# The heads' output projection in a hybrid decoder layer: input sums made two groups ahead and kept in DRAM

## The reference

```python
x = layer_norm(concatenate([meta, x_prompt]), ln_in_g, ln_in_b)
q, k, v, qi, wi, ki, hq, kf, hi, log_f, hg = project(x, w_in)
attn_o = attention of each query over its top-k keys       # 8 heads of 128
hg_o   = gated linear recurrence, normed and gated         # 8 heads of 128
mix = concatenate([attn_o, hg_o]) @ w_out
x = layer_norm(ALPHA * x + mix, ln1_g, ln1_b)
x = layer_norm(ALPHA * x + swiglu(x, w_gate, w_up, w_down), ln2_g, ln2_b)
```

## Time and profile before

| | |
|---|---|
| median of the runs | 2655.04 us (2654.91 to 2656.0) |
| the profiled execution | 2640.65 us |
| its span from the first to the last instruction | 2639.2 us |
| PE busy | 2543.4 us, 96% |
| DVE busy | 1577.6 us, 60% |
| ACT busy | 973.5 us, 37% |

### The profile page before, as it was taken

The page is one execution under the profiler, slowest core; times in us unless marked ns, Lnnn a source line. Parts: engine busy times, 40 slices in busy tenths (PEclk is TensorE's granted clock), DMA queues, the critical chain, the costliest instruction groups (busy, mean ns, idle before and its releaser), DMA issues.

```text
span 2639.2 us, 47668 instructions
## 1 busy us (share of the span) xinstructions
PE 2543.4 (96%) x20523; PEld 2479.1 (94%) x20523; DVE 1577.6 (60%) x2221; ACT 973.5 (37%) x1550; POOL 173.7 (7%) x198
## 2 busy tenths in 40 slices
PE   5999999999999899989999999999999799999996
PEld 5989999999999888989999999999999799999995
DVE  5157767776656631578777777777777433333345
ACT  5244333343333421345444444444444321212123
POOL 1111111111000112000000000000000000000002
PEclk9899999999999999989999999999999899999997
DMA  4422323333222323243333333343333543433221
GB/s 133 106 56 82 96 80 94 92 88 89 81 73 73 93 87 93 67 142 111 123 106 127 114 119 124 109 129 113 120 116 110 189 157 117 130 101 109 89 67 65
DMA packets 289965, 275.27 MB, mean 104 GB/s; under 512 B 8184, under 2 KB 266536, under 8 KB 289256
## 3 DMA queue, kind: packets, MB, share of 16 engines
q1 hardware_dynamic: 282448, 250.92, 30.7%
q0 software_dynamic: 7344, 21.80, 2.7%
HBM read 245.41 MB, written 27.29 MB: 103 GB/s over the span
## 4 chain that ended last, share of the span: by engine, by line
PE 92%; DVE 4%; ACT 3%; issue 1%; DMA 1%; SPq 0%; DVEq 0%; ACTq 0%
PE acc L1773 47%; PE acc L1373 29%; PE b L1773 5%; PE b L1357 2%; PE acc L1395 1%; PE b L1518 1%; PE b L1636 1%; PE b L1611 1%; PE b L1534 1%; PE b L1715 1%; PE b L1693 1%; PE b L1546 1%; DVE lnd L2360 1%; DMA stg<-hid_dram 1%; PE b L1637 0%
## 5 line engine op out<-in xcount | busy, mean ns | idle before, releaser
L1373 PE MATMUL acc<-xh,wh 128*128 128x260 f32 (+2 forms) x2144 | 456.5, 295 | 10.0 <-DVE xl L2234 4.5
L1373 PE MATMUL acc<-xl,wh 128*128 128x260 f32 (+2 forms) x2144 | 439.8, 287 | 0.0
L1373 PE MATMUL acc<-xh,wl 128*128 128x260 f32 (+2 forms) x2144 | 439.1, 287 | 0.0
L1230 ACT ACTIVATE ph<-pair 128x1024 fp32r<-128x1024 f32 x252 | 267.3, 1061 | 414.1 <-PE acc L1773 405.7
L1773 PE MATMUL acc<-hh,dh 128*128 128x260 f32 x1408 | 399.6, 284 | 14.8 <-DVE dl L2509 11.3
L2371 DVE TENSOR_TENSOR pl<-pair,ph 128x1024 fp32r<-128x1024 f32 x252 | 308.7, 1225 | 159.1 <-ACT ph L1230 159.1
L1773 PE MATMUL acc<-hl,dh 128*128 128x260 f32 x1408 | 399.4, 284 | 0.0
L1773 PE MATMUL acc<-hh,dl 128*128 128x260 f32 x1408 | 399.1, 283 | 0.0
L1373 PEld LDWEIGHTS acc<-xh,wh 128*128 128x128 f32 (+1 forms) x2144 | 335.1, 191 | 17.2 <-DVE xl L2234 5.6
L1373 PEld LDWEIGHTS acc<-xl,wh 128*128 128x128 f32 (+1 forms) x2144 | 336.9, 191 | 0.0
L1373 PEld LDWEIGHTS acc<-xh,wl 128*128 128x128 f32 (+1 forms) x2144 | 336.6, 191 | 0.0
(11 more groups left out here) (442 smaller groups left out, 4495.0 us busy)
## 6 DMA issues: line engine op xcount, KB each, us to landing
raw<-in_w_in_dram SPq DMA_DIRECT2D x52, 1024.0 KB, 5.7
draw<-in_w_down_dram SPq DMA_DIRECT2D x32, 1408.0 KB, 6.5
pair<-in_w_gate_dram SPq DMA_DIRECT2D x42, 1024.0 KB, 5.4
pair<-in_w_up_dram SPq DMA_DIRECT2D x42, 1024.0 KB, 5.1
raw<-in_w_out_dram SPq DMA_DIRECT2D x16, 1024.0 KB, 5.6
hid_dram<-hid SPq DMA_DIRECT2D x22, 520.0 KB, 3.2
stg<-hid_dram SPq DMA_DIRECT2D x44, 260.0 KB, 6.6
x_dram<-sacc SPq DMA_DIRECT2D x4, 1040.0 KB, 4.2
```

The costliest lines, as they stand in the source:

```text
L1230: act.activation(ph[n % 3][:, :, :], block_of(q, i), ACT.Copy).then_inc(sem("h_split"), 1)
L1373: ins = mm(acc[0:rows, t.odd, half, 0:n_], a, b[:, kx0 + k, lo + half * n_:lo + half * n_ + n_], start=(k == 0 and n == 0), stop=(k == kt ...
```

## The change

- The sums move to the end of VectorE's iterations of groups 1 and 2 in stage B, one for each of the eight products. They write two buffers `xs`, which lie where the samples' row work lies later. A sum from the third on waits until the store of the one two before has landed. The waits for the stored states go from group 3 to the first of them, as `xs` lies over those tiles; `sample_rows` waits for all eight stores.
- SP stores each sum to a new DRAM tensor `x_dram`, one after each weight load of groups 2 and 3. After the third weight load of D1 it brings the tensor back to `sacc` in two pieces of four tiles, each when those four are subtracted, the second when the first has landed.
- In D1 a tile then takes two steps: ScalarE rounds all eight, VectorE subtracts all eight. `add_mix` scales by ALPHA as it adds, for the tiles 8 to 15.
- ScalarE rounds ahead of block 11's probabilities, and takes the last product of stage B (`take(3, 3)`) behind both.
- On TensorE `pv(11)` goes behind the first product of D1, and the scores of block 12 behind the first tile of the second. The turns of block 12 stay where they are.

```diff
--- before.py
+++ after.py
@@ -280,8 +280,7 @@
     work = rb.take("work", [NS, 4, KEEP_S])
     vnew = rb.take("vnew", [NS, NG, P])
     assert rb.pos <= R_START + 29248
-    tmp = rb.take("tmp", [P, 2, NT])
-    assert rb.pos <= R_START + 33408
+    xs = at("xs", [P, 2, 2 * LIVE], F32, rb.pos - 8512)
     qpad = at("qpad", [P, NG, NS, NH], F32, R_START + 33408)
     knew = at("knew", [P, NG, NS], F32, R_START + 34432)
     assert R_START + 34432 + 128 <= TOP
@@ -393,6 +392,7 @@
     SUMS, SQ, MU, RSTD, LND = (ssum1, ssum2), (sq1, sq2), (mu1, mu2), (rstd1, rstd2), (lnd1, lnd2)
     x1_dram = nc.dram_tensor("x1_dram", (KD, P, 2 * LIVE), F32, kind="Internal")
     hid_dram = nc.dram_tensor("hid_dram", (FF // P, P, 2 * LIVE), F32, kind="Internal")
+    x_dram = nc.dram_tensor("x_dram", (8, P, 2 * LIVE), F32, kind="Internal")
     ytok = at("ytok", [P, NB + 1, D], F32, 0)
 
     acc = ctx.enter_context(nc.psum_tensor("acc", [P, 2, 2, 512], F32))
@@ -534,15 +534,30 @@
         head_loads(At(0), None)
         with sp.Fori(1, NH, 1) as h:
             head_loads(At(0, 4, h), h)
+        def keep_x(k):
+
+            sp.wait_ge(sem("x_sum"), k + 1)
+            if k:
+                sp.wait_ge(sem("x_kept"), 16 * k)
+            sp.dma_start(x_dram[k], xs[:, k % 2, :]).then_inc(sem("x_kept"), 16)
+
         for g in range(NG):
             for j, c in enumerate((W_COLS["k"] + P * g, W_COLS["v"] + P * g, 2 * P * g, 2 * P * g + P)):
                 s = At(S_B + 4 * g + j)
                 load(s, raw_at(s, KD, P), w_in3[:, :, c:c + P])
+                if g >= 2:
+                    keep_x(4 * (g - 2) + j)
         for n in range(8):
 
             s = At(S_D1 + n)
             c = (n * 256 + 1024) % D
             load(s, raw_at(s, 8, 256), wo3[:, 8:16, c:c + 256])
+            if n == 2:
+                for c4 in range(2):
+                    sp.wait_ge(sem("x_kept"), 128 + 16 * c4)
+                    sp.wait_ge(sem("mix_in"), 4 * c4 + 4)
+                    sp.dma_start(sacc[:, 8 + 4 * c4:12 + 4 * c4, S0:NT], x_dram[4 * c4:4 * c4 + 4].rearrange("k p n -> p k n"))\
+                        .then_inc(sem("x_kept"), 16)
         with sp.Fori(0, 4, 1) as n2:
             for i in range(2):
                 s = At(S_D2 + i, 2, n2)
@@ -1119,16 +1134,12 @@
                         keep_new(g - 1)
                     if j in (1, 2):
                         kv_rows(g, j - 1)
-                    att_probs(n)
+                    if n < 11:
+                        att_probs(n)
 
 
         def mix_round(k):
-            act.wait_ge(sem("x_sum"), k + 1)
             act.activation(xh[:, 8 + k, S0:NT], sacc[:, 8 + k, S0:NT], ACT.Copy).then_inc(sem("mix_h"), 1)
-
-        def mix_resid(k):
-            act.wait_ge(sem("mix_in"), k + 1)
-            act.activation(sacc[:, 8 + k, S0:NT], tmp[:, k % 2, S0:NT], ACT.Copy, scale=ALPHA).then_inc(sem("resid"), 1)
 
         def sample_att(b):
             act.wait_ge(sem("sg_turned"), b + 1)
@@ -1147,13 +1158,10 @@
         for n in range(8):
             if n == 0:
                 act.wait_ge(sem("mm"), T_D1)
-                mix_round(0)
-                for k in range(1, 9):
-                    if k < 8:
-                        mix_round(k)
-                    mix_resid(k - 1)
-                    if k == 3:
-                        take(3, 3)
+                for k in range(8):
+                    mix_round(k)
+                att_probs(11)
+                take(3, 3)
             split(At(S_D1 + n + 1))
             if n <= 4:
                 att_take(11 + n)
@@ -1724,7 +1732,12 @@
                 if n == 0 and i == 0:
                     side = {k: (mix_in(k + 1),) for k in range(7)}
                 if n <= 3:
-                    if i == 0:
+                    if n == 0 and i == 0:
+                        side[7] = (lambda: pv(11),)
+                    elif n == 0:
+                        side[0] = (lambda: att_scores(12),)
+                        side[7] = (lambda: p_turn(12),)
+                    elif i == 0:
                         side[3] = side.get(3, ()) + (lambda n=n: pv(11 + n),)
                         side[5] = side.get(5, ()) + (lambda n=n: att_scores(12 + n),)
                     else:
@@ -2195,6 +2208,11 @@
                 last = V.tensor_scalar(lg[:, hd, 0:w], lg[:, hd, 0:w], nmx[:, 1, hd:hd + 1], None, ALU.mult)
             last.then_inc(sem("att_p"), 1)
 
+        def x_sum(k):
+            if k >= 2:
+                dve.wait_ge(sem("x_kept"), 16 * (k - 1))
+            V.tensor_tensor(xs[:, k % 2, :], fr(xh[:, 8 + k, S0:NT]), fr(xl[:, 8 + k, S0:NT]), ALU.add).then_inc(sem("x_sum"), 1)
+
         q = 3 * (NH - 1)
         for g in range(NG):
             for j in range(4):
@@ -2215,20 +2233,19 @@
                         if q < KEEP_S // 8:
                             take_sample(4 * q, idx[:, 8 * q:8 * q + 8])
                             q += 1
-                    if g == 3 and j == 2:
+                    if g == 1 and j == 0:
                         dve.wait_ge(sem("sstate_out"), 16 * NH)
                         dve.wait_ge(sem("state_out"), 16 * NH)
+                    if g < 3:
+                        x_sum(4 * (g - 1) + j)
+                    if g == 3 and j == 2:
+                        dve.wait_ge(sem("x_kept"), 128)
                         sample_rows()
                     if g == 3 and j == 3:
                         dve.wait_ge(sem("rows_turned"), 1)
                         V.tensor_copy(grow[:].rearrange("p k b -> p (k b)"), b7[:, 0:16]).then_inc(sem("grow_ready"), 1)
 
 
-        def x_sum(k):
-            if k >= 2:
-                dve.wait_ge(sem("resid"), k - 1)
-            V.tensor_tensor(tmp[:, k % 2, S0:NT], fr(xh[:, 8 + k, S0:NT]), fr(xl[:, 8 + k, S0:NT]), ALU.add).then_inc(sem("x_sum"), 1)
-
         def mix_rest(k):
             dve.wait_ge(sem("mix_h"), k + 1)
             V.tensor_tensor(xl[:, 8 + k, S0:NT], sacc[:, 8 + k, S0:NT], fr(xh[:, 8 + k, S0:NT]), ALU.subtract).then_inc(sem("mix_in"), 1)
@@ -2238,7 +2255,13 @@
             t = At(T_D1 + 2 * n + i)
             m = (2 * n + i + 8) % KD
             dve.wait_ge(sem("mm"), (t + 1).v)
-            V.tensor_tensor(cut(sacc[:, m, S0:NT]), cut(sacc[:, m, S0:NT]), alive(t), ALU.add).then_inc(sem(f"acc_read{t.odd}"), 1)
+            dst = cut(sacc[:, m, S0:NT])
+            if n < 4:
+                dve.wait_ge(sem("x_kept"), 128 + 16 * (m // 4 - 1))
+                V.scalar_tensor_tensor(out=dst, in0=dst, scalar=ALPHA, in1=alive(t), op0=ALU.mult, op1=ALU.add)\
+                    .then_inc(sem(f"acc_read{t.odd}"), 1)
+            else:
+                V.tensor_tensor(dst, dst, alive(t), ALU.add).then_inc(sem(f"acc_read{t.odd}"), 1)
 
         def sample_att(b):
             dve.wait_ge(sem("slog"), b + 1)
@@ -2251,10 +2274,7 @@
 
         for n in range(8):
             if n == 0:
-                x_sum(0)
                 for k in range(8):
-                    if k < 7:
-                        x_sum(k + 1)
                     mix_rest(k)
             split(At(S_D1 + n + 1))
             if n >= 1:
```

## The result

The changed kernel takes 2638.24 us (median of 20 runs, 2628.91 to 2653.44). The kernel before, timed beside it on the same chip, takes 2658.37 (20 runs, 2641.76 to 2662.71).

A forecast was written before the change was run, and what follows sets the result against it. TensorE, busy for 96% of the span, bounds the kernel. 2.3 us (earlier start) and 6.0 (inside the ring) make 8.3, other parts nothing; off the median 2655.04 that gives 2646.7, range 2644.4 to 2650.2.

The forecast's parts named there:

- Start: Step to the output projection: rounding may begin at 871.78, first matmul 1.45 us later, 0.34 after the turns end.
- TensorE's line: Output projection: no wait after the first tile; turns of block 12 done at 889.32, before it was 897.59.
- Block 12: Attention block 12: its ScalarE and VectorE line ends by 886.5, TensorE wants it at 888.62; 2.1 us of slack.
- Sums: Eight sums of 0.70 us moved into groups 1 and 2: cost nothing, 0.36 left; uncovered 5.6 in all.
- Restoring: Stored sums' return to `sacc`: landed by 883.9, first needed by `add_mix(0,0)` at 886.5; cost nothing, 2.6 us left.
- Rival B: Start of the output projection: TensorE at the lower clock loses 2.5 us; gain 5.8, time 2649.2; chance 0.07.
- C: Block 12 becomes the bound: split as late as 884, turns wait 3.8 us, gain 4.5, time 2650.5; chance 0.09.
- D: Restored tiles late at `add_mix(0,0)`: free up to 13.5 us landing, at 27.1 slower by 5.3, 2660.3; chance 0.05.
- the sum: Whole kernel: the step's gain of 8.3 us taken off the median of 2655.04, giving 2646.7.
- the ring: Output projection before: eight tiles each sum, round, subtract and scale before `tmp` is free; TensorE waits, clock 0.72 over 873 to 879.
- the 6.0: Output projection: 6.0 us of the 8.3 gained from waiting, refilling and the lower clock inside the ring.
- the 2.3 of the earlier start: Output projection: first matmul at 873.23, not 875.55; 2.3 us of the 8.3.

The follow-up runs named there:

- keeping one wait: Changed kernel with block 11's probabilities ahead of the eight roundings again, so TensorE waits longer at the step's start: 2647.29 us (12 runs).
- the delay: Changed kernel with twelve extra tiles of full matmuls ahead of the output projection's first tile: 2650.17 us (11 runs).
- one tile shorter: Kernel before with one of 16 feature tiles left out of each of the twelve products of groups 1 to 3: 2646.41 us (7 runs).

## Why the prediction was wrong

**The steps held.** *Start*: rounding begins 0.2 us after the turns of block 11; the first output matmul comes 1.42 us later (1.45 forecast), after a wait of 0.37 (0.34). *TensorE's line*: no wait for `xl` after that, clock 1.00; the second weight tile starts at 893.05, 17.5 us after those turns began (17.5 forecast; 25.8 in the first trace of before). *Block 12*: its probabilities are ready at 890.86, 1.84 before TensorE turns them (2.1 forecast). *Sums*: VectorE's idle time before the split that had 1.06 is now 0.26 (0.36 forecast), still ended by ScalarE. *Restoring*: issued at 879.06; the two transfers took 5.1 us (median) to land, where 8.8 was taken, and VectorE goes from block 12's probabilities into `add_mix` at 890.78 without a wait. Rival B (low clock at the start), C (block 12 the bound) and D (restored tiles late) did not come. (C was priced 0.5 us too high: with a split at 884 its line of 7.89 would end at 891.9, 3.3 us behind 888.62 and not 3.8.)

```profile
695.69 2.29 DVE L1884 TENSOR_TENSOR wl<-raw,wh 128x2048 fp32r<-128x2048 f32 x1 [0.26 <-ACT wh L815]
```

**The step that failed is the sum:** "the gain is a length of waiting and of engine work, so I take it off the median". The 8.3 was read from one execution, 2640.65, that stood 0.5% below the median of the three runs beside it. The prediction saw that distance and set it aside. It was the key: the first trace shows the ring at clock 0.72 for 6 us, and the usual execution shows it at 0.50 for 15. The mis-sized term is the 6.0 for "waiting, refilling and the lower clock inside the ring": it measures 10.0 there, which with the 2.3 of the earlier start makes 12.3, not 8.3. With the sample stage steadied, the runs give 10.6 for the change. The range failed with it: its 1 us for the spread of the runs was that of three runs (2654.91 to 2656.0), while the 75 runs of before on record, these three among them, span 2640.75 to 2664.33.

**The second term was missing:** the sample stage, 101.5 us in the first trace and up to 118.4 in others of either kernel, stood in no line of the sum, as it takes no part in the change. Taking its two-column rows apart gains 13.4 us on the kernel before and 7.3 on the kernel after (means of 6 against 75 runs, and 12 against 30). So the kernel after loses some 6 us less in it. That divides the 16.8 us between the means of the two kernels into 10.6 for the step and some 6 for the sample stage; it is a division by these runs and no separate proof, and each part is uncertain by some 5 us.

**What stays open:** why the sample stage costs the kernel after less, and whether the ring reaches a stage that starts 60 us after it at all. Filling the ring's waits gained 9.1 us (4.4 to 13.8) with the samples' rows whole and 5.3 (0.6 to 10.0, on different chips) with them taken apart, where the ring's own clock accounts for 4.1; keeping one wait cost 8.2 (2.9 to 13.6), where the trace shows 3.9 of it at the step. All three are larger than the step explains, but only the first is so beyond its interval, and by little. The single traces don't bear a link out: four executions with clock 1.00 in the step had sample stages of 118.4 and 101.5 (after), 114.7 (with the delay) and 116.9 us (with the filled waits), three behind the unfilled ring 101.5, 109.4 (before) and 118.4 (one tile shorter). By what path the one would reach the other, no run shows.

## What to carry to other kernels

Before a price is read from one profiled execution, put that execution among the others, and more than three of them: where it is 0.5% off the median and its clock is higher, look in it for the stretches that ran better than usual, and price the change at both levels. A loop that feeds TensorE slower than TensorE works can cost its waits and then, as here, the lower clock on top, which hides the waits and makes TensorE look busy. Rows of very narrow matmuls are worth trying to spread among wide ones, even where no engine waits for them.

## What the runs showed of the hardware

The clock of TensorE can fall while it is busy by the trace: over the first 3.31 us of a row of 24 matmuls of two columns the granted clock was 0.88 in the mean, then 0.50 for the next 6 us, mostly of full matmuls. With the same matmuls taken apart it stayed at 1.00 in the 16 us from the first of them (the changed kernel, second run with them apart):

```profile
952.90:968.90 16.00, 16.00 (x126) 13.79 (x125) 2.23 (x7) 3.85 (x8) 3.79 (x4) 1.00 0.18 49
```

And in the usual execution the clock did not come back while the ring ran: 15 us at 0.50 with 1.09 us of waiting in three pieces and TensorE otherwise at work. In the first trace the same ring had full speed again from its third tile on (a tile in 0.99 us where it took 1.67), through waits as long or longer, so the waits alone do not settle the level:

```profile
879.57 0.51 PE L1373 MATMUL acc<-xh,wh 128*128 128x260 f32 x2 [0.34 <-DVE xl L2234]
...
881.59 0.51 PE L1373 MATMUL acc<-xh,wh 128*128 128x260 f32 x2 [1.03 <-DVE xl L2234]
```

The time of an execution followed its mean granted clock in both kernels: after at 0.984 took 2628.9 us and at 0.973 took 2653.4; before at 0.980 took 2640.75 and at 0.971 some 2664.
